# Two fused blocks on one core: the GpSimd store of a head's probabilities goes before its wait for the next table, and the gates follow the scores by three heads

## What is computed

```python
# layer A
h = rms_norm(x, a_norm); q, k, v, g = split(h @ a_w_in, 4)
sc = q_c @ k_c.T * scale + bias[rel_idx]       # per head; a banded, chunked mask
o = softmax(sc) @ v_c
x = x + (o * silu(g)) @ a_w_out
# layer B
h_kv = rms_norm(x, kv_norm); k, v = split(h_kv @ kv_w, 2)
cum = cumsum(log_sigmoid(h_kv @ f_w + f_b))    # per head
q, g = split(rms_norm(x, b_norm) @ b_w_in, 2)
sc = q @ k.T * scale + cum[q] - cum[k]         # causal
o = softmax(sc) @ v
x = x + (o * silu(g)) @ b_w_out
return rms_norm(x, final_norm)
```

## Time and profile before

| | us |
|---|---|
| runs | 2470.1, 2453.86, 2470.65 (median 2470.1) |
| profiled execution, own time | 2453.5 |
| its span | 2451.7 |
| PE busy | 2402.3 |
| DVE busy | 1790.9 |
| ACT busy | 1192.1 |
| POOL busy | 487.2 |
| mean granted TensorE clock | 0.995 of full |

### The profile page before, as it was taken

How to read it: one execution, slowest core, us unless ns; L and a number is a source line. 1 busy time by engine, 2 the same in 40 slices (tenths; PEclk the granted TensorE clock), 3 DMA queues, 4 the chain that set the end, 5 groups by cost and what they waited for, 6 DMA issues and landing times.

```text
span 2451.7 us, 40526 instructions
## 1 busy us (share of the span) xinstructions
PE 2402.3 (98%) x16396; PEld 2138.3 (87%) x16396; DVE 1790.9 (73%) x2693; ACT 1192.1 (49%) x1747; POOL 487.2 (20%) x721
## 2 busy tenths in 40 slices
PE   8999999999999999999999999999999999999998
PEld 7999999888888888888888888888888888888887
DVE  8998797996867576667667678767576767665766
ACT  6555433665444444445444456444444444444445
POOL 1212114422311021012101112321031113101311
PEclk9999999999999999999999999999999999999999
DMA  8666773486777777677767776887687778867774
GB/s 219 175 162 172 200 188 85 110 222 195 212 192 201 195 215 203 180 206 205 200 199 204 212 193 176 197 222 196 192 211 195 207 195 207 207 182 196 204 194 121
DMA packets 770633, 468.49 MB, mean 191 GB/s; under 512 B 33904, under 2 KB 726256, under 8 KB 770448
## 3 DMA queue, kind: packets, MB, share of 16 engines
q1 hardware_dynamic: 752880, 430.16, 64.8%
q0 software_dynamic: 17568, 35.75, 6.4%
HBM read 449.93 MB, written 15.89 MB: 190 GB/s over the span
## 4 chain that ended last, share of the span: by engine, by line
PE 72%; DVE 5%; issue 3%; DMA 3%; POOL 1%; ACT 1%; DVEq 0%; POOLq 0%; ACTq 0%
PE bank L295 35%; PE bank L299 17%; PE bank L326 5%; PE bank L325 5%; PE bank L329 5%; DMA pr_scratch<-sc 2%; DVE splitb L260 1%; PE bank L1917 1%; PE bank L1906 1%; PE bank L1918 1%; PE bank L1905 0%; POOL pT L1807 0%; PE bank L275 0%; PE bank L277 0%; PE bank L276 0%
## 5 line engine op out<-in xcount | busy, mean ns | idle before, releaser
L295 PE MATMUL bank<-xx,splitb 128*128 128x512 f32 x3328 | 1160.9, 395 | 10.5 <-DVE gT L2253 6.9
L260 DVE TENSOR_TENSOR splitb<-rawb,splitb 128x1024 fp32r<-128x1024 f32 x672 | 837.9, 1259 | 360.4 <-ACT splitb L254 355.6
L254 ACT ACTIVATE splitb<-rawb 128x1024 fp32r<-128x1024 f32 x672 | 700.1, 1055 | 546.1 <-PE bank L299 397.0
L299 PE MATMUL bank<-xx,splitb 128*128 128x256 f32 x3328 | 922.9, 277 | 0.8 <-DVE splitb L260 0.8
L295 PEld LDWEIGHTS bank<-xx,splitb 128*128 128x128 f32 x3328 | 628.1, 189 | 143.4 <-DVE gT L2253 7.8
L299 PEld LDWEIGHTS bank<-xx,splitb 128*128 128x128 f32 x3328 | 628.0, 189 | 3.5 <-DVE splitb L260 1.1
L295 PE MATMUL bank<-oo,splitb 128*128 128x512 f32 x1008 | 344.8, 390 | 0.0
L275 PE MATMUL bank<-xhl,splita 128*128 128x258 f32 (+1 forms) x1040 | 297.9, 286 | 11.4 <-DVE splita L260 10.2
L277 PE MATMUL bank<-xhl,splita 128*128 128x258 f32 (+1 forms) x1040 | 293.1, 282 | 0.0
L276 PE MATMUL bank<-xhl,splita 128*128 128x258 f32 (+1 forms) x1040 | 292.7, 281 | 0.0
L299 PE MATMUL bank<-oo,splitb 128*128 128x256 f32 x1008 | 278.9, 277 | 0.0
(11 more groups left out here) (298 smaller groups left out, 2380.7 us busy)
## 6 DMA issues: line engine op xcount, KB each, us to landing
rawb<-in_a_w_in_dram SPq DMA_DIRECT2D x256, 512.0 KB, 5.3
rawa<-in_w_in_dram SPq DMA_DIRECT2D x130, 512.0 KB, 5.3
rawb<-in_kv_w_dram SPq DMA_DIRECT2D x128, 512.0 KB, 4.8
rawb<-in_b_w_in_dram SPq DMA_DIRECT2D x128, 512.0 KB, 5.5
rawb<-in_a_w_out_dram SPq DMA_DIRECT2D x64, 512.0 KB, 5.3
rawb<-in_b_w_out_dram SPq DMA_DIRECT2D x64, 512.0 KB, 5.4
rawb<-in_w_out_dram SPq DMA_DIRECT2D x32, 512.0 KB, 5.0
pr_scratch<-sc POOLq DMA_DIRECT2D x64, 192.0 KB, 2.3
```

Source lines behind the costliest of these rows:

```text
L254: nc.scalar.activation(self.parts(at, h)[0], self.raw_half(at, h), ACT.Copy).then_inc(hi_ready, 1)
L260: nc.vector.tensor_tensor(lo, self.raw_half(at, h), hi.bitcast(F32), ALU.subtract).then_inc(lo_ready, 1)
L295: nc.tensor.matmul(out, hi[:, w], both(k).rearrange("p a t -> p (a t)"), start=start and k == 0, stop=False)
L299: last = nc.tensor.matmul(out[:, 0:SEQ], lo[:, w], both(k)[:, 0], start=False, stop=stop and k == 7)
```

## The change

1. `LAG` is 3. The list is now v v v v, q0 k0, q1 k1, q2 k2, q3 k3 g0, q4 k4 g1, q5 k5 g2, v v v v, q6 k6 g3, q7 k7 g4, g5, g6, g7, outputs. Three heads, not two, have their scores in a q unit. `scores(j)` from j = 3 on, and `weigh(j - 2)` with it, stand in the g unit of head j - 3. `weigh(6)` stands in the g unit of head 5, and `weigh(7)` in that of head 7.
2. POOL's `head` is cut into `ask` (issue the table's transfers) and `finish` (wait and mask), and `turn_probs` into `store` and `fetch`. The order is ask, store, finish, fetch.
3. DVE's turning of the blocks (`turn_blocks`) leaves `shares` and stands behind the evacuation of the q or g unit.
4. ACT's wait before it overwrites `vtm` is for the weighing of the head before (`o_sum`) and no longer for its gate.

```diff
-    LAG = 2
+    LAG = 3
...
-                def head(g, j):
+                def ask(g, j):
                     pool.wait_ge(sc_taken, n + 1)
...
+                def finish(g, j):
+                    n = head_no(layer, g, j)
+                    if layer == 0:
+                        pool.wait_ge(table_in, n * 16 + 16)
+                        g_.tensor_tensor(table[0:64, 0:64], table[0:64, 0:64], hidden[:], ALU.add).then_inc(table_ready, 1)
+                    else:
+                        pool.wait_ge(table_in, (n - AH) * 48 + (16 * AH + 48))
...
-                def turn_probs(g, j):
+                def store(g, j):
                     pool.wait_ge(tr_ready, n + 1)
                     if n > 1:
                         pool.wait_ge(pt_in, 16 * NQ * (n - 1))
                     pool.dma_start(pr_d[n % 2].rearrange("b r j e -> (b r) (j e)"), sc[:]).then_inc(pr_stored, 16)
+                def fetch(g, j):
                     pool.wait_ge(pr_stored, 16 * (n + 1))
                     wait(pool, o_sum, n - 1)
...
                 def heads(g):
-                    head(g, 0)
+                    ask(g, 0)
+                    finish(g, 0)
                     for j in range(GH):
                         if j < GH - 1:
-                            head(g, j + 1)
-                        turn_probs(g, j)
+                            ask(g, j + 1)
+                        store(g, j)
+                        if j < GH - 1:
+                            finish(g, j + 1)
+                        fetch(g, j)
...
                     def attend(j):
                         def emit():
-                            if j >= 2:
+                            if 2 <= j <= GH:
                                 weigh(j - 2)
+                            if j == GH + 2:
+                                weigh(GH - 1)
                             if j < GH:
                                 scores(j)
...
-                        act.wait_ge(og_ready, head_no(layer, g, b * VB) + 2)
+                        wait(act, o_sum, head_no(layer, g, b * VB))
...
                     def shares(j):
...
+                    def turn_blocks(j):
                         dve.wait_ge(p_ready, head_no(layer, g, j) * 2 + 2)
                         ...
...
                             evacuate("q", j, qT)
+                            if 1 <= j <= LAG:
+                                turn_blocks(j - 1)
...
                             evacuate("g", j - LAG, gT)
+                            if j < GH:
+                                turn_blocks(j)
                             gate(j - LAG)
```

More of the change, by code:

```diff
@@ L1779, in head @@
                         pool.dma_start(table[:, 0:SEQ], src).then_inc(table_in, 16)
-                        pool.wait_ge(table_in, n * 16 + 16)
-                        g_.tensor_tensor(table[0:64, 0:64], table[0:64, 0:64], hidden[:], ALU.add).then_inc(table_ready, 1)
-                    else:
-                        m = n - AH
-                        row = nf_d[bass.ds(m, 1), :]
+                    else:
+                        row = nf_d[bass.ds(n - AH, 1), :]
                         pool.dma_start(table[:, 0:P], row[:, 0:P].broadcast_to([P, P])).then_inc(table_in, 16)
@@ L1789, in head @@
                                        allow_slow_non_contiguous=True).then_inc(table_in, 16)
-                        pool.wait_ge(table_in, m * 48 + (16 * AH + 48))
+                def finish(g, j):
[5 more added lines that the diff above has]
+                        pool.wait_ge(table_in, (n - AH) * 48 + (16 * AH + 48))
                         v = table[:].rearrange("p (b k) -> p b k", k=P)[:, 0:3:2]
@@ L1794, in head @@
                                          ALU.add).then_inc(masked, 1)
-                def turn_probs(g, j):
+                def store(g, j):
                     n = head_no(layer, g, j)
-                    via = pr_d[n % 2]
                     pool.wait_ge(tr_ready, n + 1)
@@ L1802, in turn_probs @@
                         pool.wait_ge(pt_in, 16 * NQ * (n - 1))
-                    pool.dma_start(via.rearrange("b r j e -> (b r) (j e)"), sc[:]).then_inc(pr_stored, 16)
+                    pool.dma_start(pr_d[n % 2].rearrange("b r j e -> (b r) (j e)"), sc[:]).then_inc(pr_stored, 16)
+                def fetch(g, j):
+                    n = head_no(layer, g, j)
                     pool.wait_ge(pr_stored, 16 * (n + 1))
@@ L1807, in turn_probs @@
                         pool.dma_start(pT[n % 2][QB * b:QB * b + QB, :].rearrange("r (b e) -> r b e", b=NQ),
-                                       via[:, :, b].rearrange("b r e -> r b e")).then_inc(pt_in, 16)
+                                       pr_d[n % 2, :, :, b].rearrange("b r e -> r b e")).then_inc(pt_in, 16)
                 def scale_pair(m):
```

## The result

The changed kernel takes 2430.5 us (median of six runs, 2427.3 to 2431.8) against 2455.8 us for the kernel before (2453.7 to 2470.7): a ratio of 0.988 with a 95% interval of 0.986 to 0.991. The forecast was 2440 us in a range of 2425 to 2458, and 2435 us for the profiled execution, which took 2430.6 us; its span went from 2451.7 to 2428.9 us. The forecast started from a median of 2470.1 us in three runs before; the 2455.8 us are the median of six.

A forecast was written before the change was run, and what follows sets the result against it. PE, busy 98%, was taken as the bound, with only its waits and slow clock to win. Terms 11.9 + 15.0 + 1.2 - 10.0 = 18.1 us off 2453.5 gave 2435.4; about 5 us for run differences made 2440, range 2425 to 2458.

The forecast's parts named there:

- The ledger: List of PE's waits in the attention layers, 20.8 us in all, with 8.5 us of slow clock added.
- slow stretches: Times at about half clock behind PE stalls of 1.88 us or more; five in the layers, 1.7 us each.
- the kT waits: Five PE waits for kT before `scores`, 2.4 us in all; half was expected to go, gain 1.2 us.
- the new wait: PE before `weigh(6)` in g5, waiting for `gate(4)`: 1.25 us in each of eight groups, 10.0 us lost.
- PE's filling: About 0.15 us that PE needs to fill again after each of fifteen stalls; named, not in the sum.
- weigh(7): PE's 8.5 us of waits on the memory round trip go, with two slow stretches: gain 11.9 us, margin 1.2 us.
- The store ahead of the table: POOL in layer 1 stores about 5.5 us sooner; 9.9 us of PE waits and three slow stretches go: gain 15.0 us.
- Rival A: Store queued behind the table's transfers takes its full 5.8 us more, so layer 1 gains nothing: 2450 us, chance 0.13.
- the bound I read from the rows: Slow stretches were seen behind PE stalls of 1.88 us or more, none behind 1.75 and 1.85 us.
- B: Rival: no PE wait before `weigh(6)`, the gate's result being there in time; 10 us more go, 2425 us, chance 0.15.
- C: Rival: waits before `weigh(6)` of 2.5 to 3 us, each setting off a slow stretch; 2463 us, chance 0.07.
- D: Rival: POOL is late for other reasons, or the runs' 16.6 us above the profiled execution stay whole; 2452 us, chance 0.10.

## Why the prediction was right

**The ledger.** PE's idle time and slow stretches were nearly the whole account. The sum said 18.1 us, measured were 22.9 us in the profiled execution. Of the 4.8 us more, 1.2 us are the kT waits, of which I had kept half and none stayed, and 0.4 us are the new wait, 9.6 us and not 10.0. The idle time fell from 20.8 to 9.6 us and the clock gave back 8.5 us, 19.7 us together. The last 3 us are in neither view. PE's filling, which I had named and left out of the sum, makes 1 us of it at my 0.15 us a stall, with seven stalls fewer. The other 2 us are open.

**How the median came out.** The forecast of 2440 us lay 9.5 us too high: 4.8 us from the sum, and about 5 us that I had added for the spread of the runs and that did not come. The range held both.

**weigh(7).** Gone, as forecast, but I gave its margin from the wrong cost. The later turning is not worth 0.9 us: it moves the fetch beside a weight load and costs 4 us of landing. In the third group of the changed kernel the fetches have a median of 4.0 us to landing. In the kernel with the late turning and `LAG` 2 PE got the data 17.3 to 17.8 us behind the scores; in the changed kernel `weigh(7)` stands at 19.1 us. The margin was there, 1.3 us and more, for two reasons that I had not counted. First, the worst wait of before had such a collision in it already: SP issued a load at 2150.41, ahead of the fourth fetch at 2150.65. Its four fetches, and then those of the third group, where PE did not wait:

```profile
DMA to landing us min/median/max: 2.1/2.7/4.8
DMA to landing us min/median/max: 2.1/2.1/2.2
```

Second, the new wait before `weigh(6)` holds `weigh(7)` back by its own 1.15 to 1.26 us. Without it, in the kernel with `weigh(6)` in g6, the seventh group has 0.1 us left. So the margin of 1.2 us came out right partly by luck.

**The store ahead of the table.** Right, and larger than forecast: I gave it 15.0 us, and alone it took 20.6 us off the profiled execution. This step carries the result (2431.7 us), and without it nothing is left (2464.0 us). The other steps were forecast at 11.9 - 10.0 = 1.9 us and gave 1.2 us, which is within the spread of the runs. Stores to landing in the changed kernel:

```profile
DMA to landing us min/median/max: 2.2/2.3/4.7
```

The store at 1999.98 behind a table asked for at 1996.04 took 4.3 us and landed about 1 us after the last of the table's transfers, 11.8 us behind its scores, where the prediction had 10 to 11 at the low end. The first head of the other seven groups has the same weight load issued 0.8 us behind its store; there the table landed earlier, at most 2.2 us behind the store's issue and not 3.3, and the store took 2.3 to 2.9 us. That fits the section "Two DMAs through the same engine are not ordered" of the Trainium skill's page "DMA: Bandwidth & Descriptors", by which descriptors of one queue of a DMA engine start in order. The page adds that they are pipelined, so the prediction's step from there, that the store moves its bytes only when the table's are read, says more than the page does. It is one late case; the order itself was not tried. Rival A still falls: the next scores come 11.6 us behind, and `maxima` reads `sc` another 2.5 us later (2006.58 us).

Of the working, one term does not follow: the third and fourth scores were put 9.8 + 1.2 = 11.0 us apart, and `maxima` was then said to want `sc` at 11.8 us. The trace has them 11.2 us apart, and the store between them landed 9.0 to 10.0 us behind the third scores, so nothing hung on it.

**The new wait.** 1.15 us (layer 0) and 1.26 us (layer 1) idle in each of eight groups, 1.25 forecast. Without a slow stretch, as forecast, though the bound I read from the rows was no bound.

**Rivals.** B was excluded by the eight waits. C needs waits of about 3 us; made that long they cost 20.5 us in the time, and the kernel was still 0.3% faster than before. D was wrong in its second half: I let 5 us of the difference between the runs stand and gave 0.10 to all of it staying. The changed kernel's six runs lie within 4.5 us. Those of the kernel before lie within 17 us, and within 25 us in all that were taken beside the experiments.

I had put that spread down to stalls that hang on a landing and the slow stretches behind them. The runs fit this only in part. The kernels with no long wait spread little (2418.3 to 2420.7 us, 2420.3 to 2422.0 us), those with a late store much (2457.1 to 2468.4 us with the store after the table). But with `weigh(6)` before the first pair, where a gate and not a landing releases PE, the runs lie within 5.8 us, and with the late turning and `LAG` 2, where a landing does so eight times, within 6.4 us. The cause of the spread stays open.

## What to carry to other kernels

Where one engine is busy 98%, list its idle gaps and its slow stretches, find for each the last thing that was late, and ask what a reordering puts next to what: this change removed 20.8 us of waits and set up eight new ones (9.6 us) whose size could be read from the trace before. Then ask whether a new wait can be had for nothing: moving one weighing by a unit took these away. On a queue that issues and waits, issue all that is ready before waiting for anything. A small transfer on the critical path should be issued ahead of the next large load, and if it cannot be, hold the load back: 0.86 us of delay cost 42 us here, and one wait on the loading queue gave it back.

## What was not expected of the hardware

- Four fetches of 48 KB landed in 2.1 us (median) ahead of a 1 MB load and in 4.5 us where its issue fell between them; the slowest of the four took 2.9 and 6.9 us.
- Stalls of PE of 2.85 us were followed by a stretch at half clock in the four groups of layer 0 and stalls of 2.95 us in none of the four of layer 1, within one execution. In another kernel, both in layer 1, a stall of 1.96 us was followed by one and a stall of 2.59 us was not.
- In the kernel with the late turning and LAG 2 every one of eight stalls of 4.9 to 5.4 us was followed by half clock.
